# A two-block transformer stack on one core: l2 sums of sixteen heads in four column groups

## What is computed

```python
def _l2norm(x):
    return x * lax.rsqrt(jnp.sum(x * x, axis=-1, keepdims=True) + EPS)
...
    q = q.reshape(B_, T_, GDN_HEADS, GDN_DK).astype(jnp.float32)
    k = k.reshape(B_, T_, GDN_HEADS, GDN_DK).astype(jnp.float32)
...
    q = _l2norm(q) * (GDN_DK ** -0.5)
    k = _l2norm(k)
```

## Time and profile before

| | |
|---|---|
| median of 3 runs | 1268.21 us (1267.95 to 1268.28) |
| span of the profiled execution | 1268.2 us |
| TensorE busy | 1254.3 us, 99% |
| VectorE busy | 919.6 us, 73% |
| ScalarE busy | 699.2 us, 55% |
| mean share of the 16 DMA engines, main queue | 46.9% |

### The profile page before, as it was taken

The page is one execution under the profiler, slowest core; times in us unless marked ns, Lnnn a source line. Parts: engine busy times, 40 slices in busy tenths (PEclk is TensorE's granted clock), DMA queues, the critical chain, the costliest instruction groups (busy, mean ns, idle before and its releaser), DMA issues.

```text
span 1268.2 us, 23324 instructions
## 1 busy us (share of the span) xinstructions
PE 1254.3 (99%) x9041; PEld 1169.6 (92%) x9041; DVE 919.6 (73%) x1290; ACT 699.2 (55%) x1082; POOL 154.3 (12%) x113
## 2 busy tenths in 40 slices
PE   9999999999999999999999999999999999999998
PEld 8997999999989998889998989999889998999986
DVE  6886874878778774447734547999758777999954
ACT  5556465654456343345354546666547567766642
POOL 0000142000000000000000001642200000464310
PEclk9999999999999999999999999999999999999999
DMA  7552332322355555555553444555564444454562
GB/s 300 189 173 101 133 134 101 133 68 68 152 197 188 195 179 185 198 170 182 183 209 109 156 173 167 198 169 195 194 221 171 162 154 163 167 188 175 197 224 93
DMA packets 30315, 212.83 MB, mean 168 GB/s; under 512 B 3488, under 2 KB 3616, under 8 KB 5152
## 3 DMA queue, kind: packets, MB, share of 16 engines
q1 hardware_dynamic: 29088, 206.53, 46.9%
q0 software_dynamic: 1152, 5.24, 1.1%
HBM read 210.71 MB, written 1.05 MB: 167 GB/s over the span
## 4 chain that ended last, share of the span: by engine, by line
PE 86%; DVE 8%; ACT 4%; DMA 1%; issue 1%; SPq 0%; DVEq 0%; ACTq 0%
PE lin L540 50%; PE lin L702 21%; DVE wlo L513 3%; PE lin L2883 2%; PE lin L567 2%; ACT whi L506 2%; PE lin L569 1%; DMA raw<-in_stream 1%; PE aux L2627 1%; PE aux L2599 1%; PE aux L2485 1%; ACT lm L1377 1%; PE aux L725 1%; PE aux L2745 1%; PE aux L2555 1%
## 5 line engine op out<-in xcount | busy, mean ns | idle before, releaser
L513 DVE TENSOR_TENSOR wlo<-raw,whi 128x2048 fp32r<-128x2048 f32 x183 | 427.4, 2338 | 170.8 <-ACT whi L506 170.1
L506 ACT CAST whi<-raw 128x2048 fp32r<-128x2048 f32 x192 | 365.3, 1906 | 179.5 <-DMA raw<-in_stream 147.0
L540 PE MATMUL lin<-xhi,whi 128*128 128x256 f32 (+2 forms) x1616 | 461.5, 286 | 1.0 <-DVE wlo L513 1.0
L540 PE MATMUL lin<-xlo,whi 128*128 128x256 f32 (+2 forms) x1616 | 457.0, 283 | 0.0
L540 PE MATMUL lin<-xhi,wlo 128*128 128x256 f32 (+2 forms) x1616 | 454.7, 281 | 0.0
L540 PEld LDWEIGHTS lin<-xhi,whi 128*128 128x128 f32 x1616 | 304.1, 188 | 3.0 <-DVE wlo L513 1.2
L540 PEld LDWEIGHTS lin<-xhi,wlo 128*128 128x128 f32 x1616 | 306.1, 189 | 0.0
L540 PEld LDWEIGHTS lin<-xlo,whi 128*128 128x128 f32 x1616 | 304.6, 189 | 0.4
L865 POOL TENSOR_TENSOR fu<-fs,ft 128x256 f32<-128x256 f32 x44 | 86.2, 1958 | 259.4 <-ACT fs L1479 259.4
L2292 DVE SCALAR_TENSOR_TENSOR ft<-fy,par,ft 128x254 f32<-128x254 f32 (+1 forms) x176 | 109.5, 661 | 5.9 <-DVE ft L2292 0.2
L540 PE MATMUL lin<-whi,xhi 128*128 128x256 f32 x256 | 74.2, 290 | 0.0
(11 more groups left out here) (454 smaller groups left out, 2123.2 us busy)
## 6 DMA issues: line engine op xcount, KB each, us to landing
raw<-in_stream SPq DMA_DIRECT2D x193, 1024.0 KB, 4.9
gp<-in_gains POOLq DMA_DIRECT2D x6, 512.0 KB, 3.9
c<-in_const SPq DMA_DIRECT2D x1, 1460.0 KB, 16.0
h<-in_x SPq DMA_DIRECT2D x2, 544.0 KB, 4.4
c<-in_const POOLq DMA_DIRECT2D x1, 1024.0 KB, 6.5
ht<-in_xtok POOLq DMA_DIRECT2D x1, 1024.0 KB, 9.6
out<-ht SPq DMA_DIRECT2D x1, 512.0 KB, 2.6
out<-ht SPq DMA_DIRECT2D x2, 256.0 KB, 2.0
```

The lines of the kernel that those rows point to most:

```text
L506: nc.scalar.copy(whi[:, s0 % 4], raw[:, s0 % 4]).then_inc(hi_ready, 1)
L513: nc.vector.tensor_tensor(wlo[:, s0 % 4], raw[:, s0 % 4], whi[:, s0 % 4].bitcast(F32), ALU.subtract).then_inc(lo_ready, 1)
L540: ins = nc.tensor.matmul(out, a, b, start=start and n == 0, stop=stop and n == 2)
```

## The change

The sixteen matmuls stay sixteen, of the same 272 or 256 columns, but they write four groups of 32 output rows: heads 2j and 2j + 1 add into the rows 32j to 32j + 31, the keys into rows 32j and 32j + 1, the queries into rows 32j + 2 and 32j + 3, and the other 28 rows of a group get zeros. The order goes round the groups: four consecutive matmuls belong to four groups. A window is now 32 columns wide, so the constant has 40 columns, with ones in column 3. What follows handles 128 rows: ScalarE copies 128 rows into rstd, the three transposes take 128 rows and write 128 columns each, and VectorE picks two of every 32 columns, for which it needs five instructions in place of three. The eight more constant columns move every tile that lies behind c1 by 32 bytes.

```diff
-CONST1 = [("ident", 128), ("window", 32), ("upper", 128), ("upper16", 128), ("ones16", 128), ("spread", 128), ("head", 8),
+CONST1 = [("ident", 128), ("window", 40), ("upper", 128), ("upper16", 128), ("ones16", 128), ("spread", 128), ("head", 8),
...
-                    is_free(nc.scalar.copy(rhead[0:16, 0:T1], b[0:16, 0:T1]), "l2sum")
+                    is_free(nc.scalar.copy(rstd[:], b[:, 0:T1]), "l2sum")
...
                 b = full(dve, "l2t")
-                nc.vector.tensor_scalar(kmeta, b[0:META, 40:48], EPS, None, ALU.add)
-                nc.vector.tensor_scalar(gqn[:], wide(b[:, 0:32], 16)[:, :, 0:8], EPS, P * P * EPS, ALU.add, ALU.mult)
-                is_free(nc.vector.tensor_scalar(knorm[:, 0:16].rearrange("p (c n) -> p c n", n=8),
-                                                wide(b[:, 0:32], 16)[:, :, 8:16], EPS, None, ALU.add), "l2t")
+                def of(rows, c, lo):
+                    return b[0:rows, c * P:c * P + P].rearrange("p (j r) -> p j r", r=32)[:, :, lo:lo + 2]
+
+                nc.vector.tensor_scalar(kmeta.rearrange("p (j i) -> p j i", i=2), of(META, 2, 0), EPS, None, ALU.add)
+                for c in range(2):
+                    nc.vector.tensor_scalar(gqn[:, c].rearrange("p (j i) -> p j i", i=2), of(P, c, 2), EPS, P * P * EPS,
+                                            ALU.add, ALU.mult)
+                    ins = nc.vector.tensor_scalar(knorm[:, 8 * c:8 * c + 8].rearrange("p (j i) -> p j i", i=2), of(P, c, 0),
+                                                  EPS, None, ALU.add)
+                is_free(ins, "l2t")
...
-                    ins = nc.tensor.transpose(b[0:m, 16 * c:16 * c + 16], rhead[0:16, t0:t0 + m], ident[0:16, 0:16])
+                    ins = nc.tensor.transpose(b[0:m, c * P:c * P + P], rstd[:, t0:t0 + m], ident)
...
-            for n in (*range(8, 16), *range(8)):
-                src, t0 = (sqk, 0) if n >= 8 else (sqq, META)
-                a = CCOL["window"] + 15 - n
-                ins = nc.tensor.matmul(b[0:16, t0:T1], c1[:, a:a + 16], src[:, n % 8, t0:T1], start=n == 8, stop=n == 7)
+            for i in range(4):
+                src, t0 = (sqk, 0) if i < 2 else (sqq, META)
+                a = CCOL["window"] + 3 - i
+                for j in range(4):
+                    ins = nc.tensor.matmul(b[32 * j:32 * j + 32, t0:T1], c1[:, a:a + 32], src[:, 2 * j + i % 2, t0:T1],
+                                           start=i == 0, stop=i == 3)
...
-    c = {"ident": np.eye(P), "window": np.tile(np.arange(32) == 15, (P, 1)), "upper": up, "upper16": up & same16, "ones16": same16,
+    c = {"ident": np.eye(P), "window": np.tile(np.arange(40) == 3, (P, 1)), "upper": up, "upper16": up & same16, "ones16": same16,
```

More of the change, by code:

```diff
@@ L189, in program @@
         gss = nxt("gss", [P, 2, 8])
-        rhead = rstd[0:16]
         spare = PCOL["conv"]
```

## The result

The changed kernel takes 1259.03 us (median of 5 runs, 1258.08 to 1260.18) against 1267.95 us (1267.46 to 1268.28) for the kernel before, a ratio of 0.9929 with a 95% interval of 0.9918 to 0.9941. I had forecast 1264.9 us, 3.3 us gained, with a range of 1262.9 to 1266.8.

A forecast was written before the change was run, and what follows sets the result against it. The prediction took TensorE, busy 99% of 1268.2 us, as the bound. Removing VectorE's 3.45 us wait, less 0.16 for extra VectorE instructions, gave 3.3 us: 1268.2 - 3.3 = 1264.9 us, range 1262.9 to 1266.8.

The forecast's parts named there:

- The sums: Sixteen l2 matmuls on TensorE: four groups overlap, so they take 1.95 us instead of 7.3 and end 5.3 us sooner.
- D: Rival at the sums: weight loads stand alone between matmuls, adding 3.1 us; 1.85 us gained, 1266.4 us; chance 0.08.
- E: Rival at the sums: groups run one by one, still 7.3 us, plus 0.4 us behind them; 1268.6 us; chance 0.07.
- F: Rival at the sums: the array empties at every group change, sums take 12.3 us; 1273.6 us; chance 0.03.
- The cover and the path: Behind the sums: VectorE's wlo ends at 116.63, capping the gain at 3.45 us; less 0.16, 3.3 us net.
- Whether it lasts: From "ak" to the end: later work shifts whole and nothing gives the 3.3 us back.
- The 32 bytes: Tiles behind the constants: the wider window moves them 32 bytes, costed at nothing.
- The base of the sum: Whole kernel: profiled span 1268.2 us and runs' median 1268.21 agree, so the gain is subtracted from 1268.2.
- The clock: TensorE around "ak": whether the fall to half clock, costing 1.6 us, persists after the change.
- once before and once after: Main case: the clock still falls once in "ak", 1.6 us before and after; 1264.9 us; chance 0.45.
- gone: Clock rival at "ak": the fall vanishes with the narrow sums, another 1.6 us gained; 1263.3 us; chance 0.30.

The follow-up runs named there:

- l4: The kernel before with the tiles behind the constants moved 64 bytes further; 1267.36 us, ratio 0.9994.
- l2: The changed kernel with the same tiles moved another 32 bytes further; 1265.81 us, ratio 0.9981.
- g1: The changed kernel with the sums finishing one column group before starting the next; 1258.20 us, ratio 0.9921.
- l1: The kernel before with every activation 32 bytes further on and no column groups; 1260.18 us, ratio 0.9938.
- k3: The changed kernel with activations 64 bytes further and seven unread matmuls filling TensorE's wait for VectorE; 1256.15 us, ratio 0.9908.
- h4: The kernel before with all its memory, weights and activations, 32 bytes further; 1267.68 us (one run).
- g2: The changed kernel with the sums going round two column groups, then round the other two; 1258.19 us, ratio 0.9920.
- h3: The changed kernel with its tiles another 64 bytes further; 1256.21 us (one run).

## Why the prediction was wrong, step by step

- **The sums: right.** 1.95 us forecast, 2.0 measured. Four column groups ran side by side, so D (loads that stand alone), E (groups one by one) and F (an array that empties) all fell. The rule behind D, of the Trainium skill ("TensorE: Matmul & The Clock Gate", Part 3), as the prediction reads it, is not borne out: all four groups use all rows, and the 32 loads lie hidden (0.90 us of load time within the 2.0).
- **The cover and the path: right.** VectorE's wlo bounds the gain. 3.3 us forecast; 3.4 in the profile after and 3.4 between l4 and l2. Two groups were as good as four, as said, although their sums took 2.9 us and not 3.7. Beyond the cover the loss begins as said: the 4.8 us of g1 cost 1.3.
- **Whether it lasts: right.** Of 3.4 us, 0.1 to 0.2 are given back by the end.
- **The 32 bytes: this step failed.** The prediction says of them "I cost at nothing" and "no row tells whether addresses matter". They are worth 8.0 us, more than twice the path (l1), and this term alone takes the time out of the range. A row hints at it in hindsight: the three tiles of a 512-column product, of the same shape, last 392, 394 and 399 ns in the kernel before. Where the operand alone makes 7 ns of difference, its place may. The bound that was missing is simple: some 400 such groups, three records each; if each record gains or loses those few ns, that is 5 to 8 us either way, and the range should have held it.
- **The base of the sum.** I took the span of the profiled execution as the runs' time because both read 1268.2. A run's time is its span plus 1.8 us (1257.2 and 1259.03 after). The profiled execution of before was longer than the runs, 1270.0 by that count, with a half-clock stretch that at least 39 of 46 runs did not have by their mean clock. The sum loses nothing by it, since 1268.2 is the runs' median too; the reading that the typical run has the stretch was wrong.
- **The clock.** I gave 0.45 to "once before and once after" and 0.30 to "gone". It was the reverse of the second: for the typical run it came with the change. The reason I gave against it, the empty wait that grows to 1.9 us in one piece, is the one that k3 partly supports. Beside a base without the stretch this step misses 1.5 us and more, in the other direction.

Together: 1268.0, less 8.0 for the place, less 3.4 for the path, is 1256.6, where the runs without a stretch lie. The medians 1258.85 and 1259.03 lie 2.3 and 2.4 above, which I put down to the clock: one stretch costs 1.5, the long one 3.0. From profile to profile both have a stretch. The lead of 11.3 us at the last fhi, 11.9 without the late start, is 3.4 for the path and 8.5 for the rest, half a microsecond more than l1's median gave for the place. That half belongs to the profiled execution of before: h4, with the same pace of the 512-column records, gains 0.65 us on it between 130 and the end, and l1 gains 8.5 on it there. So place and path add up.

## What to carry to other kernels

An edit that moves memory touches every instruction that uses what lies behind it. Cost it by their number times the smallest difference the records show between equal shapes, and run it alone. Where a serial piece is shortened, find what stands ahead of the next engine's part before you count the gain, and look whether the wait that appears goes with a fall of the clock. Compare a profiled execution's clock with that of the timed runs before you take it as typical.

## What the runs showed of the hardware

- **Distance between the operands' tiles.** With the weights moving and the activations stationary, three 512-column fp32r records take 701, 687, 700.5 and 681 ns where the activations lie 32, 64, 96 and 0 bytes (remainder by 128) behind the weights. Moving both together changes nothing (h4). The 256-column records don't follow this distance alone.
- **Column groups in fp32.** Sixteen two-record matmuls with all rows take 2.0 us in four groups of 32 columns and 7.3 us on the same 16 columns, 3.6 times as long. A matmul of the next group may start beside one that stands ahead of it in the program (g1), so the order of the groups counts for less than their number.
- **The clock differs between executions of one kernel.** The changed kernel showed half-clock stretches (0.50 of full speed) of 3.4 and 6.8 us in two profiles; g2 and h3, with waits of 0.8 and 1.6 us in the same place, none there.
